# Three reorderings in a one-core decoder step: bias table in four column groups, row sums of x inside the projections, gate and memory heads later

## What is computed

```python
z = einsum("bsd,dc->bsc", rms_norm(x, g_mix), w_in)        # one projection, 9 chunks of 512 columns
uv = gelu(z[..., :1024]); u, va = uv[..., :512], rms_norm(uv[..., 512:], g_av)
qb, kb = rms_norm(q, g_qb), rms_norm(k, g_kb); qm = rms_norm(z[..., 4096:], g_qm)
ya = u * (tril(w_s) @ va + b_s)                             # spatial gate, 4 groups of 128 channels
yb = dilated_attend(qb, kb, vb, rel_bias)                   # bias = rel_bias[t5_bucket(distance)]
mk, mv = rms_norm(kv[..., :512], g_km), kv[..., 512:]       # kv = rms_norm(mem, g_mem) @ w_mem_kv
ym = memory_attend(qm, mk, mv)                              # 4 heads over 256 memory tokens
h = x + concat(ya, yb, ym) @ w_out
y = h + hier_moe(rms_norm(h, g_ffn))                        # 32 experts, two per token
```

## Time and profile before

| | us |
|---|---|
| median of three runs (lowest, highest) | 1157.11 (1155.02, 1161.47) |
| profiled execution, own time | 1158.69 |
| its span, first to last instruction | 1156.8 |
| TensorE busy in the span | 1063.6 (92%) |
| VectorE busy | 550.7 (48%) |
| ScalarE busy | 200.7 (17%) |
| GpSimd busy | 41.1 (4%) |

### The profile page before, as it was taken

One profiled execution on the slowest core, in us unless ns is written; L12 is line 12 of the kernel. 1 busy time (PEld: TensorE's weight loads), 2 busy tenths in 40 slices (PEclk: granted clock), 3 DMA queues, 4 the chain that ended last, 5 costly groups with the idle time before them and its releaser, 6 DMA issues.

```text
span 1156.8 us, 17254 instructions
## 1 busy us (share of the span) xinstructions
PE 1063.6 (92%) x7153; PEld 590.5 (51%) x7153; DVE 550.7 (48%) x1078; ACT 200.7 (17%) x457; POOL 41.1 (4%) x38
## 2 busy tenths in 40 slices
PE   8999999999999999989999998999998969797966
PEld 3587776666666665667777542333332323232322
DVE  3585554664455454574435116544443434343423
ACT  1111103221212231301011021111211111111110
POOL 0021010001100000000000000000000000000000
PEclk9899999999999998999999999999999999999996
DMA  9989439899999997732866448999999999999993
GB/s 319 363 237 358 152 133 391 341 359 350 347 404 397 369 368 273 299 120 87 309 258 253 183 162 373 429 412 429 426 427 428 426 429 428 428 430 425 429 426 121
DMA packets 38612, 384.53 MB, mean 332 GB/s; under 512 B 4863, under 2 KB 7551, under 8 KB 10207
## 3 DMA queue, kind: packets, MB, share of 16 engines
q1 hardware_dynamic: 35968, 375.83, 81.1%
q0 software_dynamic: 1568, 5.62, 1.8%
q10 hardware_dynamic: 1008, 2.10, 0.6%
HBM read 375.63 MB, written 7.90 MB: 332 GB/s over the span
## 4 chain that ended last, share of the span: by engine, by line
PE 72%; DMA 14%; DVE 9%; issue 2%; ACT 1%; POOL 1%; ACTq 0%; DVEq 0%; SPq 0%; POOLq 0%
PE ps L605 24%; DMA arena<-w_gu 12%; PE ps L597 7%; PE ps L1026 6%; PE ps L1003 5%; PE ps L1057 5%; PE ps L1041 4%; PE ps L800 4%; PE ps L587 3%; PE ps L767 3%; DMA arena<-w_proj 2%; DVE cst L1788 1%; PE ps L1062 1%; DVE cst L1727 1%; PE ps L783 1%
## 5 line engine op out<-in xcount | busy, mean ns | idle before, releaser
L605 PE MATMUL ps<-arena 128*128 128x256 f32 x1456 | 338.5, 388 | 0.1
L605 PEld LDWEIGHTS ps<-arena 128*128 128x128 f32 x1456 | 274.3, 193 | 52.4 <-issue 14.4
L1026 PE MATMUL ps<-arena,cst 128*32 128x512 f32 x1024 | 122.5, 613 | 30.6 <-DMA arena<-w_gu 28.8
L1788 DVE STREAM_TRANSPOSE cst<-ps 128x512 f32<-128x512 f32 x31 | 22.2, 717 | 172.2 <-PE ps L1003 172.2
L597 PE MATMUL ps<-arena 128*64 128x256 f32 x832 | 101.3, 385 | 0.0
L1003 PE MATMUL ps<-arena,cst 128*32 128x512 f32 (+1 forms) x768 | 94.5, 605 | 0.5 <-DVE cst L1723 0.5
L1026 PEld LDWEIGHTS ps<-arena,cst 128*32 128x32 f32 x1024 | 32.1, 111 | 114.9 <-issue 79.7
L1041 PE MATMUL ps<-arena,stat 128*32 128x512 f32 x512 | 68.1, 653 | 23.8 <-DVE stat L1792 23.8
L597 PEld LDWEIGHTS ps<-arena 128*64 128x64 f32 x832 | 55.1, 136 | 38.0 <-issue 14.4
L1057 PE MATMUL ps<-arena,cst 128*128 128x512 f32 x128 | 58.6, 611 | 9.5 <-ACT cst L1268 9.5
L1810 DVE COPY arena<-ps 32x512 f32<-32x512 f32 x64 | 44.2, 691 | 47.3 <-PE ps L1041 45.9
(11 more groups left out here) (261 smaller groups left out, 982.2 us busy)
## 6 DMA issues: line engine op xcount, KB each, us to landing
arena<-w_gu SPq DMA_DIRECT2D x64, 2048.0 KB, 28.8
arena<-w_dn SPq DMA_DIRECT2D x32, 2048.0 KB, 27.1
arena<-w_proj SPq DMA_DIRECT2D x43, 1024.0 KB, 7.6
arena<-kc SPq DMA_DIRECT2D x16, 2048.0 KB, 10.6
arena<-vc SPq DMA_DIRECT2D x16, 2048.0 KB, 9.2
arena<-w_o SPq DMA_DIRECT2D x16, 1024.0 KB, 4.8
arena<-kc SPq DMA_DIRECT2D x8, 1024.0 KB, 8.2
arena<-vc SPq DMA_DIRECT2D x8, 1024.0 KB, 9.9
```

What stands on the lines that cost most here:

```text
L605: last = mm(psum[:, regions(v)[j - 1]], left[a], right[:, a], start=first and opens and a == 0, stop=final and a == 1, skip_group_check=True)
L1026: last = mm(ps[g:g + 32, 0, :], xgT[:, s % 2, kt, :], w[:, k, :], start=kt < 4, stop=kt >= KT - 4)
```

## The change

The table's first four products go into bank 6 at partitions 0, 32, 64 and 96, with one semaphore step after the fourth; the fifth goes into bank 2. Step 4 no longer waits for the copies, since its regions lie in other banks. The tiles of x are loaded after weights 10 (tiles 0 and 1) and after unit 5 (tile 2) instead of in the memory steps; their squares come on ScalarE after the memory values are scaled; their means are made on VectorE at s = 9 and their root is a third `rsqrt` on GpSimd, ahead of those of the norms. ScalarE waits for that root at s = 11. The key loads of the first sample sequence, which write over `xst`, come three units later. GATE_AT goes from 102 to 104, MHEAD_AT and the last four TURN_AT entries go one unit later.

```diff
-GATE_AT = 102
+GATE_AT = 104
-MHEAD_AT = (92, 94, 96, 98)
+MHEAD_AT = (93, 95, 97, 99)
-TURN_AT = [..., 90, 90, 91, 91]
+TURN_AT = [..., 91, 91, 92, 92]
...
 # SP
-            x_tile(0)
-            x_tile(1)
             x_columns(1)
             sp.wait_ge(unit_done, 8)
             weights(6)
             x_columns(2)
             x_columns(3)
-            x_tile(2)
             for i in (7, 8, 9, 10):
...
+            x_tile(0)
+            x_tile(1)
...
                 if s == 5:
+                    x_tile(2)
                     sp.wait_ge(tab_out, 16)
...
-                if s in (8, 11, 14):
+                if s in (11, 14, 17):
                     sp.wait_ge(sumsq, 5)
-                    keys(0, s // 3 - 2)
+                    keys(0, s // 3 - 3)
...
 # TensorE
-                    if q == 0:
-                        pe.wait_ge(tab_cp, 4)
                     mixed_products(i, 0, memT, q, mem_mix, q == 0, q == QTR - 1)
                 if i == QTR - 1:
                     pe.wait_ge(s_relb, 32)
-                    for n in range(TABLE // 512):
-                        if n >= 2:
-                            pe.wait_ge(tab_cp, n - 1)
-                        mm(ps[0:H, 6 + n % 2, :], relb[:, :], onehot[:, n * 512:(n + 1) * 512], start=True, stop=True).then_inc(tab_mm, 1)
+                    for n in range(4):
+                        last = mm(ps[32 * n:32 * n + H, 6, :], relb[:, :], onehot[:, n * 512:(n + 1) * 512], start=True, stop=True)
+                    last.then_inc(tab_mm, 1)
+                    mm(ps[0:H, 2, :], relb[:, :], onehot[:, 4 * 512:TABLE], start=True, stop=True).then_inc(tab_mm, 1)
...
 # ScalarE
-            for n, (m, col) in enumerate(tiles):
-                act.wait_ge(s_xst[n % 2], 16 * (n // 2 + 1 + (n == 4)))
-                nc.scalar.activation(xst[0:m, n % 2], xst[0:m, n % 2], ACT.Square, accum_out=stat[0:m, col:col + 1]).then_inc(sumsq, 1)
+            for n in range(2):
+                tile_sums(n, NORM_MEM + n)
...
+            for t in range(3):
+                tile_sums(2 + t, NORM_X + t)
...
+                if s == 11:
+                    act.wait_ge(rs_ready, 3)
                 if s % 12 == 11:
                     evict(s // 12)
...
 # VectorE
-                dve.wait_ge(tab_mm, n + 1)
-                V.tensor_copy(table[:, n * 512:(n + 1) * 512], ps[0:H, 6 + n % 2, :]).then_inc(tab_cp, 1)
+                dve.wait_ge(tab_mm, 1 + n // 4)
+                g = 32 * (n % 4)
+                V.tensor_copy(table[:, n * 512:(n + 1) * 512], ps[g:g + H, 6 if n < 4 else 2, :]).then_inc(tab_cp, 1)
...
-            dve.wait_ge(sumsq, 5)
-            V.tensor_scalar(stat[:, 0:5], stat[:, 0:5], 1.0 / D, EPS, ALU.mult, ALU.add).then_inc(ms_ready, 1)
+            dve.wait_ge(sumsq, 2)
+            V.tensor_scalar(mem_sums, mem_sums, 1.0 / D, EPS, ALU.mult, ALU.add).then_inc(ms_ready, 1)
...
+                if s == 9:
+                    x_sums = stat[:, NORM_X:NORM_X + 3]
+                    dve.wait_ge(sumsq, 5)
+                    V.tensor_scalar(x_sums, x_sums, 1.0 / D, EPS, ALU.mult, ALU.add).then_inc(ms_ready, 1)
+                    state["n"] += 1
...
 # GpSimd
-            rsqrt(1, st_rs[:, 0:5], stat[:, 0:5])
+            rsqrt(1, st_rs[:, NORM_MEM:NORM_MEM + 2], stat[:, NORM_MEM:NORM_MEM + 2])
...
-            rsqrt(3, st_nr[:, 0:24], st_n[:, 0:24])
+            rsqrt(3, st_rs[:, NORM_X:NORM_X + 3], stat[:, NORM_X:NORM_X + 3])
             rsqrt(4, st_nr[:, 0:24], st_n[:, 0:24])
```

More of the change, by code:

```diff
@@ L57 @@
 MEM_AT = 94
-GATE_AT = 102
+GATE_AT = 104
 PAIR_AT = (37, 41, 45, 49, 71, 75, 79, 83)
-MHEAD_AT = (92, 94, 96, 98)
+MHEAD_AT = (93, 95, 97, 99)
 NORM_AT = (4, 13, 25, 49, 61, 85, 97)
-TURN_AT = [10, 11, 12, 13, 19, 20, 21, 22, 30, 31, 32, 33, 61, 61, 62, 62, 66, 66, 67, 67, 90, 90, 91, 91]
+TURN_AT = [10, 11, 12, 13, 19, 20, 21, 22, 30, 31, 32, 33, 61, 61, 62, 62, 66, 66, 67, 67, 91, 91, 92, 92]
 def place(h):
@@ L1089, in _ @@
             memory_quarter(3)
-            tiles = [(P, NORM_MEM), (P, NORM_MEM + 1)] + [(P, NORM_X + t) for t in range(len(ROWS))]
+            def tile_sums(n, col):
+                act.wait_ge(s_xst[n % 2], 16 * (n // 2 + 1 + (n == 4)))
+                nc.scalar.activation(xst[:, n % 2], xst[:, n % 2], ACT.Square, accum_out=stat[:, col:col + 1]).then_inc(sumsq, 1)
             act.wait_ge(dset, 1)
-            for n, (m, col) in enumerate(tiles):
-                act.wait_ge(s_xst[n % 2], 16 * (n // 2 + 1 + (n == 4)))
-                nc.scalar.activation(xst[0:m, n % 2], xst[0:m, n % 2], ACT.Square, accum_out=stat[0:m, col:col + 1]).then_inc(sumsq, 1)
+            for n in range(2):
+                tile_sums(n, NORM_MEM + n)
             act.wait_ge(rs_ready, 1)
@@ L1372, in _ @@
             mix_weights(7)
-            dve.wait_ge(sumsq, 5)
-            V.tensor_scalar(stat[:, 0:5], stat[:, 0:5], 1.0 / D, EPS, ALU.mult, ALU.add).then_inc(ms_ready, 1)
+            mem_sums = stat[:, NORM_MEM:NORM_MEM + 2]
+            dve.wait_ge(sumsq, 2)
+            V.tensor_scalar(mem_sums, mem_sums, 1.0 / D, EPS, ALU.mult, ALU.add).then_inc(ms_ready, 1)
             x_quarter(2)
@@ L1869, in _ @@
             pool.dma_start(o_mk.rearrange("(t p) n -> p t n", p=P), mk).then_inc(st_mem, 16)
-            rsqrt(3, st_nr[:, 0:24], st_n[:, 0:24])
+            rsqrt(3, st_rs[:, NORM_X:NORM_X + 3], stat[:, NORM_X:NORM_X + 3])
             rsqrt(4, st_nr[:, 0:24], st_n[:, 0:24])
+            rsqrt(5, st_nr[:, 0:24], st_n[:, 0:24])
             pool.wait_ge(normed, 3)
@@ L1875, in _ @@
             store_v(0)
-            rsqrt(5, st_nr[:, 0:24], st_n[:, 0:24])
             rsqrt(6, st_nr[:, 0:24], st_n[:, 0:24])
+            rsqrt(7, st_nr[:, 0:24], st_n[:, 0:24])
             pool.wait_ge(normed, 5)
@@ L1881, in _ @@
             store_v(1)
-            rsqrt(7, st_nr[:, 0:12], st_n[:, 0:12])
             rsqrt(8, st_nr[:, 0:12], st_n[:, 0:12])
+            rsqrt(9, st_nr[:, 0:12], st_n[:, 0:12])
             pool.wait_ge(normed, 7)
@@ L1886, in _ @@
             pool.dma_start(o_va[128:192, :], z[0:64, Z_VA, 2, :]).then_inc(st_va, 16)
-            rsqrt(9, st_hr[:, 0:3], st_h[:, 0:3])
+            rsqrt(10, st_hr[:, 0:3], st_h[:, 0:3])
 def distance_bucket(dist):
```

## The result

The changed kernel took 1141.04 us in the median of 4 runs (1139.58 to 1143.33), the kernel before 1157.07 beside it (1155.02 to 1161.47). The ratio is 0.9864, 95% interval [0.9846, 0.9883], so some 16 us less; forecast were 1138.7 and a range of 1135.0 to 1147.5. The profiled execution took 1141.11 us with a span of 1139.2, 17.6 less than the span before.

The account below looks back on a forecast made before the run. TensorE, busy 92% of the span, was taken as the bound, so only its holes and half clock could be won. Savings of 6.4 + 4.8 + 1.1 + 5.4 + 0.7 = 18.4 us gave 1138.7 us, range 1135 to 1147.5.

Parts of the forecast that it names:

- Table: Bias table between memory steps 3 and 4: column groups remove copy waits and half clock, 6.4 us saved.
- The rival that the groups don't overlap: Bias table: column groups run one after another and the clock still falls, leaving 0.7 us gain; 1144.4 us, chance 0.05.
- Rows of x later: Moving x tile loads out of the memory steps: worth 0 at the old place, price 0 at the new.
- Worth 0: Old place, ahead of weights 6 and 7: removing x loads gains nothing, since TensorE waited for no weights there.
- Price 0 taken: Tile 2 after s = 5: lands about 91, before the 92.7 limit; late bound 4.0 us plus about 1.8 half clock.
- the first rival: Before s = 12 or 13: tile 2 lands late and TensorE waits; gain 12.6 us, 1144.5 us, chance 0.17.
- weights 13 from s = 15, so that is free: SP's queue behind tile 2: weights 13, first used at s = 15, can wait there at no cost.
- Late steps: s = 90 to 107: query turns 4.8, memory heads 1.1, gate 5.4, first gate turn 0.7; together 12.0 us saved.
- The second rival: Heads, query turns and gate meet new VectorE waits; gains at s = 90 to 107 halve to 6.0; 1144.7 us, chance 0.10.
- What is won reaches the end: Expert stage: its weight stream starts when TensorE frees slots, so an earlier mixer moves the whole stage earlier.
- That rival: Expert stage is held by its weight stream and takes back the mixer's gain: no change, 1157 us, chance 0.04.
- the blocked queue: Slower case: tile 2 lands far later, the wait at s = 12 eats everything; 1166 us at 120, chance 0.04.

Follow-up runs that it names:

- the run with the heads back: Changed kernel with MHEAD_AT back at 92, 94, 96, 98 and the last four query turns all at 91; 1140.06 us, ratio 0.9868.
- The version with tiles 0 and 1 early: Changed kernel with x tiles 0 and 1 loaded ahead of weights 6 again, only tile 2 moved; 1136.83 us, ratio 0.9836; repeated 1137.69 us, 0.9849.
- the table alone: Kernel before with only the table's products in column groups and no copy waits, x rows and late steps as before; 1157.2 us, ratio 1.0006.
- all but the x move: Changed kernel with the x rows loaded and summed as in the kernel before; 1145.86 us, ratio 0.9898.

## Why the prediction came out as it did

The time was 2.3 us above the forecast and inside its own range. By the prediction's steps:

**Table: right.** 6.4 us forecast, 6.49 in A. Products of 1.8 us (1.81), eight records in column groups at the price of the sample scores (36.59 to 37.45 is 0.86, forecast 0.93), copies hidden by 0.6 (0.71), clock at 1.00. With the old table's A of 38.46 to 38.88 the gain is 6.1 to 6.5. The rival that the groups don't overlap is out.

**"Rows of x later": wrong in both of its prices.** The step that failed first is "Worth 0: ... TensorE waited for no weights there". That no wait was there is true and is not slack: TensorE came to weights 7 only 1.4 us after they had landed, because the stop and the half clock at the table had held it back. The table's 6.4 are there only because tile 2 leaves the queue; without that they are gone (1.0006). That the sum came out all the same is luck: both edits are in the change, and the step was wrong. The prediction asked what is late next for VectorE and TensorE, but not for the transfers, and it left out the middle of the chain, where the answer stood.

The second is "Price 0 taken" at the new place: 2.33 us, between 0 and the late bound of 5.8. Tile 2 was expected at about 91 and landed at 93.48, for the dry place in the queue had moved (0 GB/s from 56 to 57 in the changed kernel): tile 0 left SP at 63.25 and landed at 78.5, in a stretch of 66 to 289 GB/s in which GpSimd's stores of the table run. Tile 2 goes into the same buffer, so SP held it back 1.1 us until tile 0 was squared, and issued it at 80.56. That was the first rival's mechanism at a fifth of its price of 5.8 (1.19 us, the loss between s = 11 and s = 14).

The third is "weights 13 from s = 15, so that is free". Their first reader is VectorE's mix at s = 13, not TensorE at s = 15. They came 3.56 us after VectorE was ready, and the rest of the chain to TensorE cost 1.13 us between s = 17 and s = 20.

**Late steps: right.** 4.8 forecast for the query turns, 4.66 by the run with the heads back; 1.1 for the heads, 1.58; 5.4 and 0.7 for the gate and its first turn, together 6.1, against 6.49 from s = 101 to s = 110 in that run (35.69 to 29.20). In all 12.0 forecast, 12.72 measured against one profile of the kernel before; the four profiles with the old steps give 11.6 to 14.1, so no error of this forecast is shown. The second rival, new waits for old, is out: of such waits the 0.91 and 0.38 shown above are all, and the 0.38 is a head turn, which the prediction wanted free of waits.

**What is won reaches the end: right.** 472.35 and 472.14 us from s = 155 on, and 469.4 to 474.1 in all profiles. That rival is out too, and the blocked queue was nowhere near.

So 18.4 forecast is 16.9 measured from the table to the end: 19.2 without the loss in B, less 2.33. The version with tiles 0 and 1 early measures the same 19.2 (647.39 - 628.2), against the same one profile of the kernel before.

## What to carry to other kernels

That an engine does not wait for a transfer says nothing on how late it could come: before a stall ahead of it is taken away, follow the chain of waits through the next stretch, and where it passes through a transfer, the gain can end there unless what stands in front of it in the queue goes too. An edit priced at nothing can be the condition of another edit's gain, so price each one with and without the others. And look for the first reader of a load on every engine: here it was VectorE's mix, two steps ahead of TensorE.

## What the runs showed of the hardware

Two things were not expected. With x tile 2 in front (64 rows, loaded twice into 64 partitions each) the queue moved about 150 to 250 GB/s at a DMA share near 1.0, from 50 to 59 us in three profiles (the kernel before, the table alone, all but the x move), where the weights around it move at over 400; in the latter two TensorE then waited 6.75 and 4.71 us. Two tiles of 1 MB over 128 partitions cost nothing, but they stood elsewhere, ahead of weights 6, at 398 to 442 GB/s from 28 to 49 us in the run with tiles 0 and 1 early. A tile over 128 partitions in the place of tile 2 was not run, so how much of the wait comes from the 64 partitions, and how much from 1 MB at this place, stays open.

And stores took the DMA engines from everything else. The stores of `table`, eight of 128.5 KB, each 16 rows of 8224 bytes, are issued by GpSimd from 59.9 to 63.8 us. From 61 to 66 us GpSimd's queue (q0) moved 0.52 MB and kept the engines at a share of 97.5%, about 104 GB/s, while the queue of the weights and x tiles (q1) moved nothing, although weights (issued at 62.88) and x tile 0 (63.25) stood in it. That tile took 15.3 us to land, against a median of 5.9 us for weights of the same size issued between 28 and 66 us.

```profile
q0 software_dynamic: 112, 0.52, 97.5%
q1 hardware_dynamic: 6, 0.00, 0.1%
...
arena<-w_proj SPq DMA_DIRECT2D x6, 1024.0 KB, 5.9
...
bias_q_d<-arena POOLq DMA_DIRECT2D x8, 128.5 KB, 6.3
arena<-x_rows SPq DMA_DIRECT2D x1, 1024.0 KB, 15.3
```

(DMA of the changed kernel. First the queues from 61 to 66 us: packets, MB, share of 16 engines; then the issues from 28 to 66 us: count, KB each, median us from issue to landing.)
